# Expert weights in one transfer of 48 KB rows, with the opening and the attention laid out anew, in a two-layer decoder

## The chip, the cores and the metric

One NeuronCore of a Trainium2 chip runs the whole program in one launch. The metric is the device time in microseconds. TensorE (PE) multiplies, VectorE (DVE) and ScalarE (ACT) work element by element, GpSimd (POOL) builds constants, and SyncE (SP) issues nearly all DMAs; they meet through semaphores. 16 DMA engines move the data from HBM into the on-chip memory of 128 partitions.

## What is computed

Two layers over a stream of 256 tokens by 1024 values, all in float32:

```
for l in range(2):
    h = rms_norm(x, norm_mix[l])
    if l == 0:   # u, v, q, k, vv = split(h @ even_w_in)
        a_out = gelu(u) * (tril(W_s) @ norm(gelu(v)) + b)      # 8 groups of 64, chunks of 128 tokens
        b_out = stick_breaking_attention(q, k, vv)             # 8 heads of 64
        mix = concat(a_out, b_out) @ even_w_out
    else:        # gate_b, gate_c, h2 = split(h @ odd_w_in)
        mix = (gate_b * conv3(gate_c * h2)) @ odd_w_out
    x = x + mix
    x = x + hierarchical_moe(rms_norm(x, norm_ffn[l]), ...)
out = rms_norm(x, norm_final)
```

The attention weight of query t on key s < t is sigmoid(z_ts) times the product of (1 - sigmoid(z_tj)) over s < j < t. It is worked out as exp of z minus sums of softplus. The mixture picks one of 4 groups and in it 2 of 8 experts for each token. An expert has three weights, gate and up (1024 x 512) and down (512 x 1024), 2 MB each: `out += combine * ((silu(t @ w_gate[e]) * (t @ w_up[e])) @ w_down[e])`. All 32 experts of a layer are loaded and computed, each for up to 32 tokens gathered by rank; further blocks exist for experts with more tokens.

## The kernel before

Each engine has one program, written out by hand, and semaphores order them.

**The ring.** A ring of 9 places (`RING`) holds one weight matrix of 2 MB each, 16 KB per partition (`SLOT`). Every matrix has a number n and goes to place n % 9. SyncE issues the loads in the order of use (`fill`, `first`, `expert`, `experts`, L330 to L408). Each load waits until the matrix that held the place is used up: `gate_used`, `gu_ready` or `y_ready` for the three matrices of an expert (`used_up`). PE waits for each matrix by itself (`wait_landed`).

**The expert stage** (`moe` and `expert` of each engine). A turn is three experts (`TRI`), and 27 experts run in a hardware loop of 9 turns (`TURNS`). Expert 27 (`EARLY`) has its gate and up weights in other buffers and its down weights in `spare`, all loaded ahead. Experts 27 to 31 are written out. The last one's down matrix comes in four transfers. PE's order within an expert: gate products (L1449, 64 records), up products (64), scatter of the expert before (L1466), turning of the selection (L1472), gather for the next expert (L1478), down products (L1458, 32 records).

```
for mat, used in enumerate((gate_used, gu_ready, y_ready)):
    n = L_MOE[l] + 3 * i + mat
    sp.wait_ge(used, after(l, e - TRI))
    load(n, matrix(l, e, mat), buffer(n, mat))
```

**The mixers.** Projections use split float32: ScalarE rounds a weight to fp32r (`hi`, L530), VectorE makes the rest (`lo`, L782), and PE adds three fp32r products (L1278 for channels, L1323 for tokens, L1339 for the output). A high part lies two places back in the ring. Layer 0 starts on five pieces of the transposed x and of the first weight matrix (`PIECES`, L427 and L343), so that PE can start early. Its attention goes in two halves of four heads: `scores` (L1370), `clip` (L864), exp and ln (L613, L618), `softplus` with a mask (L870, L872), `suffixes` (L1379 to L1381, full precision), `lows` (minimum with a mask, L879), exp (L625, L626), `values` (L1392). The v branch and the gating products (L1419) run between. Four loads of the first experts wait for the mixer's end: `even_lo` and `out_half` in layer 0, `pb_ready` and `out_half` in layer 1.

Of the kernel before, what the change touches and what calls it, by code (L numbers as in the profile page):

```python
# [50 lines left out]
L_MOE = [7, 7 + PER_MOE + 8]  # L51
L_ODD = 7 + PER_MOE
L_GAIN = L_MOE[1] + PER_MOE
LAST_DOWN = L_ODD - 1
APART = [L_EVEN, L_EVEN + 1, LAST_DOWN, L_ODD]
# [3 lines left out]
SPLIT = [L_EVEN + i for i in range(7)] + [L_ODD + i for i in range(8)]  # L59

# [18 lines left out]
def trunk(nc, x_in, x_turned_in, even_w_in, even_w_out, gmlp_w_s, gmlp_b_s, columns, odd_w_in,  # L79
          odd_w_out, norm_gains, router, w_gate, w_up, w_down, norm_final, out):  # L80
    with ExitStack() as ctx:
# [21 lines left out]
        att = [scr[:, 2048 + 384 * i:2048 + 384 * (i + 1)] for i in range(4)]  # L103
# [33 lines left out]
        def temp(cols):  # L137
# [29 lines left out]
        ident, below, upto, nlin, nones, diag = (sb(n, P) for n in (  # L167
            "ident", "below", "upto", "nlin", "nones", "diag"))
        below16, ones16 = sb("below16", P, BF16), sb("ones16", P, BF16)
# [21 lines left out]
        bank = [psum[:, i, :] for i in range(8)]  # L191
        GU, YB, XB, BB = bank[4], bank[5], bank[6], bank[7]


        landed = [sem(f"landed{i}") for i in range(RING)]
        gate_used, out_half = sem("gate_used"), sem("out_half")
# [35 lines left out]
        s_ready, low_ready, a_ready = sem("s_ready"), sem("low_ready"), sem("a_ready")  # L232
# [23 lines left out]
        def slot(n):  # L256
            return ring[:, (n % RING) * SLOT:(n % RING + 1) * SLOT]
# [8 lines left out]
        def lo_slot(n):  # L266
            return slot_halves[n % RING][:, :]
# [4 lines left out]
        def used_up(n):  # L272

            for l in range(2):
# [12 lines left out]
        def is_split(n):  # L287
            return L_EVEN <= n < L_MOE[0] or L_ODD <= n < L_MOE[1]

        def wait_landed(eng, n, turns=0):  # L290

            apart = sum(n > z and n % RING == z % RING for z in APART)
            eng.wait_ge(landed[n % RING], (turns + (n // RING + 1 - apart)) * 16)
# [26 lines left out]
        def rest_entry(l, e):  # L320
            return L_MOE[l] + 3 * e - 3


# [4 lines left out]
        def _(sp):  # L328
            def load(n, src, dst):
                sp.dma_start(dst, src).then_inc(landed[n % RING], 16)  # L330
# [8 lines left out]

            def load_piece(n, src, part, landed_of):  # L340
                ks = pieces(n)[part]
                ks = slice(ks.start, ks.stop)
                sp.dma_start(wide(n)[:, ks, :], src[:, ks, :]).then_inc(landed_of[part], 16)  # L343

            def load_early(l, i, part, parts):

                w = (w_gate, w_up)[i][l, EARLY].rearrange("(p k) f -> p k f", k=K)
# [6 lines left out]
            def load_spare(l):  # L354
                if l:
                    sp.wait_ge(y_ready, after(l - 1, EARLY))
                sp.dma_start(spare, w_down[l, EARLY].rearrange("(p j) d -> p j d", p=P)).then_inc(spare_landed, 16)

            def matrix(l, e, mat):
                w = (w_gate, w_up, w_down)[mat][l, e]  # L360
                return w.rearrange("(p j) d -> p j d", p=P) if mat == 2 else w.rearrange("(p k) f -> p k f", k=K)
# [8 lines left out]
            def expert(l, b, i):  # L370
                e = b * TRI + i
                for mat, used in enumerate((gate_used, gu_ready, y_ready)):
                    n = L_MOE[l] + 3 * i + mat
                    sp.wait_ge(used, after(l, e - TRI))
                    load(n, matrix(l, e, mat), buffer(n, mat))

            def experts(l):
                first(l, 0, 0)
                if l == 0:
                    first(l, 0, 1)  # L380
                load_spare(l)
                if l == 1:
                    first(l, 0, 1)
# [1249 lines left out]
```

## Time and profile before

| | us |
|---|---|
| median of 3 runs | 1086.62 |
| lowest, highest | 1085.47, 1086.83 |
| profiled execution | 1086.43 |
| its span | 1084.3 |

| engine | busy us | share of the span |
|---|---|---|
| PE products | 814.4 | 75% |
| PE weight loads | 637.4 | 59% |
| DVE | 321.6 | 30% |
| ACT | 192.3 | 18% |
| DMA queue 1 (SyncE's loads) | | 95.9% of 16 engines |

The page gives each engine's busy time, the span in 40 slices and the chain of work that ended last. That chain holds DMA for 63% and PE for 30%. A wait named "issue" is time in which an engine waited for nothing that the profile shows. A timeline row has the start, the duration, the engine and the line, then in brackets the idle time before it and what ended it. The profiled execution took 2.1 us more than its span; that part is not in the trace.

### The profile page before, as it was taken

The page shows a single profiled execution, that of the slowest core. Times are in us where ns is not written, and L with a number is a line of the kernel's source. Part 1 is how long each engine was busy: PE and PEld are TensorE (multiplying, and loading weights), DVE is VectorE, ACT ScalarE, POOL GpSimd, SP SyncE. Part 2 cuts the span into 40 slices and gives each one's busy share as a digit, 9 for nine tenths or more (in the row PEclk, how much of TensorE's full clock was granted, in tenths as well). Part 3 has the DMA queues.
Part 4 walks back from the last instruction along what each step waited for, and adds up shares of the span by engine and source line. Part 5 has one row for each costly group of instructions (what it writes and reads, how often), then busy time and mean ns, then how long its engine had stood idle before and what let it go on. Part 6 is the DMA issues. An engine that isn't in the chain of part 4 may idle for free.

```text
span 1084.3 us, 30469 instructions
## 1 busy us (share of the span) xinstructions
PE 814.4 (75%) x13924; PEld 637.4 (59%) x13925; DVE 321.6 (30%) x801; ACT 192.3 (18%) x367; POOL 4.9 (0%) x24
## 2 busy tenths in 40 slices
PE   8999887666676766686799998966676767676864
PEld 8887665444454545464489986754454545454642
DVE  5765522111111101121177744311111111111212
ACT  5665211000000000000163331100000000000102
POOL 1000000000000000000000000000000000000000
PEclk9999999898978888888999989988978888889988
DMA  9976999999999999999998599999999999999996
GB/s 350 426 304 257 418 427 427 429 429 429 428 429 429 428 427 430 428 427 426 417 429 368 214 400 394 430 426 430 428 428 429 429 428 428 430 428 427 429 422 254
DMA packets 35872, 439.62 MB, mean 405 GB/s; under 512 B 4208, under 2 KB 4976, under 8 KB 9968
## 3 DMA queue, kind: packets, MB, share of 16 engines
q1 hardware_dynamic: 34848, 437.58, 95.9%
q10 hardware_dynamic: 976, 1.33, 0.4%
q8 instruction: 39, 0.64, 0.2%
q14 instruction: 9, 0.07, 0.0%
HBM read 437.84 MB, written 1.05 MB: 405 GB/s over the span
## 4 chain that ended last, share of the span: by engine, by line
DMA 63%; PE 30%; DVE 3%; issue 2%; ACT 1%; SPq 0%; ACTq 0%; DVEq 0%
DMA ring<-in_w_up 32%; DMA ring<-in_w_down 30%; PE psum L1278 8%; PE psum L1449 7%; PE psum L1339 4%; PE psum L1458 4%; PE psum L1323 2%; PE psum L1466 1%; PE psum L1478 1%; PE psum L1257 1%; DMA ring<-in_even_w_in 1%; PE psum L1530 1%; DVE ring_halves L782 1%; PE psum L1472 0%; PE psum L1250 0%
## 5 line engine op out<-in xcount | busy, mean ns | idle before, releaser
L1449 PE MATMUL psum<-ring,m 128*32 128x128 f32 x7936 | 310.6, 321 | 231.3 <-DMA ring<-in_w_gate 109.9
L1449 PEld LDWEIGHTS psum<-ring,m 128*32 128x32 f32 x7936 | 272.2, 130 | 277.0 <-issue 125.1
L1143 DVE TENSOR_TENSOR m<-psum,m 128x128 f32<-128x128 f32 x64 | 18.7, 292 | 575.5 <-ACT m L683 575.5
L1458 PE MATMUL psum<-ring,m 128*32 128x256 f32 x1984 | 120.8, 380 | 15.3 <-DMA ring<-in_w_down 12.1
L683 ACT ACTIVATE m<-psum 128x128 f32<-128x128 f32 x64 | 17.7, 277 | 530.1 <-PE psum L1449 530.1
L1278 PE MATMUL psum<-scr_halves,ring_halves 128*128 128x256 f32 x768 | 107.0, 286 | 4.4 <-DVE ring_halves L782 3.8
L1278 PEld LDWEIGHTS psum<-scr_halves,ring_halves 128*128 128x128 f32 x768 | 100.9, 194 | 5.0 <-DVE ring_halves L782 4.2
L1458 PEld LDWEIGHTS psum<-ring,m 128*32 128x32 f32 x1984 | 66.2, 110 | 62.1 <-issue 21.9
L1466 PE MATMUL psum<-m 32*128 32x256 f32 x1056 | 80.7, 422 | 2.1 <-DVE m L1148 1.1
L782 DVE TENSOR_TENSOR ring_halves<-ring,ring_halves 128x2048 fp32r<-128x2048 f32 (+2 forms) x37 | 68.6, 1885 | 11.6 <-ACT ring_halves L530 11.3
L1478 PE MATMUL psum<-x,m 128*32 128x256 f32 x1024 | 69.8, 385 | 2.2 <-issue 1.5
L530 ACT ACTIVATE ring_halves<-ring 128x2048 fp32r<-128x2048 f32 (+2 forms) x37 | 57.3, 1581 | 38.7 <-PE psum L1278 28.8
L1466 PEld LDWEIGHTS psum<-m 32*128 32x128 f32 x1056 | 51.3, 199 | 21.3 <-issue 14.8
L1117 DVE STREAM_TRANSPOSE m<-psum 128x256 f32<-128x256 f32 x64 | 28.8, 450 | 91.3 <-PE psum L1478 91.3
L689 ACT ACTIVATE m<-psum 128x256 f32<-128x256 f32 x62 | 23.8, 383 | 169.0 <-PE psum L1458 169.0
L1478 PEld LDWEIGHTS psum<-x,m 128*32 128x32 f32 x1024 | 27.1, 109 | 25.6 <-issue 13.3
L1126 DVE TENSOR_SCALAR m<-count,pos,cw 128x128 f32<-128x128 f32 x128 | 38.3, 342 | 1.2 <-issue 1.2
L685 ACT ACTIVATE m<-psum 128x256 f32<-128x256 f32 x64 | 24.5, 383 | 73.8 <-PE psum L1472 73.7
L1339 PE MATMUL psum<-ring_halves,aux_halves 128*128 128x512 f32 x96 | 32.7, 395 | 0.0
L1112 DVE TENSOR_SCALAR m<-count,pos,rstd 128x32 f32<-128x32 f32 x128 | 32.2, 296 | 0.8 <-DVE extra L1100 0.7
L1472 PE MATMUL psum<-ident,m 128*128 128x128 f32 x128 | 28.0, 300 | 0.0
L1120 DVE TENSOR_TENSOR m<-m,gains 128x256 f32<-128x256 f32 x64 | 27.2, 425 | 2.2
(188 smaller groups left out, 498.4 us busy)
## 6 DMA issues: line engine op xcount, KB each, us to landing
ring<-in_w_gate SPq DMA_DIRECT2D x62, 2048.0 KB, 40.5
ring<-in_w_up SPq DMA_DIRECT2D x62, 2048.0 KB, 40.7
ring<-in_w_down SPq DMA_DIRECT2D x60, 2048.0 KB, 41.1
ring<-in_odd_w_in SPq DMA_DIRECT2D x5, 2048.0 KB, 26.2
ring<-in_even_w_in SPq DMA_DIRECT2D x3, 2048.0 KB, 20.5
ring<-in_even_w_out SPq DMA_DIRECT2D x2, 2048.0 KB, 30.8
spare<-in_w_down SPq DMA_DIRECT2D x2, 2048.0 KB, 23.2
ring<-in_w_down SPq DMA_DIRECT2D x8, 512.0 KB, 37.6
```

Source lines behind the costliest of these rows:

```text
L530: act.activation(hi_slot(n)[:, c], slot(n)[:, c], ACT.Copy).then_inc(w_hi, 1)
L782: dve.tensor_tensor(lo_slot(n)[:, c], slot(n)[:, c], hi_slot(n)[:, c].bitcast(F32), ALU.subtract).then_inc(w_lo, 1)
L1112: last = dve.tensor_scalar(sel[:, t, CAP * i:CAP * (i + 1)], ranks, pos[:, bass.ds(at(e, t), 1)], rstd[:, t:t + 1], ALU.is_equal, ALU.mult)
L1117: return dve.transpose(xg[:, i, :, :], XB[:, 0:DP].rearrange("p (q k) -> p k q", k=K))
L1126: last = dve.tensor_scalar(wsel[:, t, :].rearrange("p (n c) -> p n c", n=NP), count[:, 1:CAP + 1].unsqueeze(1).to_broadcast([P, NP, CAP]), ...
L1278: return pe.matmul(bank[banks[c // 2]][:, (c % 2) * S:(c % 2 + 1) * S], w[a][:, k, P * c:P * (c + 1)], h[b][:, k, :], start=k == 0 and a + ...
L1339: last = pe.matmul(bank[2 * t + c][:, :], mix[a][:, 4 * r + j, P * t:P * (t + 1)], w[b][:, j, 512 * c:512 * (c + 1)], start=r == 0 and j = ...
L1449: last = pe.matmul(GU[CAP * part:CAP * (part + 1), lo:lo + FP], block_of(k), w_of(k)[:, FP * part:FP * (part + 1)], start=k == 0, stop=k = ...
L1458: last = pe.matmul(YB[CAP * part:CAP * (part + 1), 0:DP], hhT[:, CAP * f:CAP * (f + 1)], w[:, f, DP * part:DP * (part + 1)], start=f == 0, ...
L1466: last = pe.matmul(bank[part][:, DP * t:DP * (t + 1)], cmb[r, P * t:P * (t + 1)], yy[r, :], start=False, stop=False, skip_group_check=True)
L1472: last = pe.transpose(BB[:, P * t:P * (t + 1)], wsel[:, t, :], ident[:, :])
L1478: last = pe.matmul(XB[CAP * part:CAP * (part + 1), 0:DP], sel[:, t, CAP * i:CAP * (i + 1)], x[:, t, DP * part:DP * (part + 1)], start=t == ...
```

## The change

**Expert weights.** The three matrices of an expert lie side by side in HBM, 48 KB for each partition. The ring's places shift by two, so that an expert takes three places in a row, and one entry of the ring (`HOLE`) stays unused between the odd mixer and layer 1's experts. From the third turn on (expert 6) an expert comes in one transfer that waits for `y_ready` of the expert that held its places; PE waits once. Turns 0 and 1, expert 27 and expert 31 keep one transfer for each matrix. PE's first turn is written out ahead of its loop.

**Sources.** The pieces of x, of the first two weights of layer 0, of the first of layer 1 and of the last down matrices lie contiguous in HBM.

**Attention.** Its blocks are laid out by key block and head parity, over 512 columns, in three pieces of four heads (`LATE` is the diagonal block of the second 128 keys). The causal mask goes into the scores as a product with `ident16` and `diag16` (bf16), so the masking passes of VectorE go. The later block's softplus is split (`low_hi`, `low_lo`) and its suffix sums are fp32r products. The scores run between the two halves of vv, the suffixes between the halves of v and ahead of the last quarter of u. `hi(5)` and `lo(5)` move behind the second exp and ln.

```diff
-L_MOE = [7, 7 + PER_MOE + 8]
+L_MOE = [7, 7 + PER_MOE + 9]
+HOLE = L_ODD + 8
+def place(n):
+    return (n + 2) % RING
+def is_whole(e):
+    return FINE <= e < NE - 1 and e != EARLY
...
+            def whole(l, e, i, former):
+                sp.wait_ge(y_ready, after(l, former))
+                at = place(L_MOE[l] + 3 * i) * SLOT
+                sp.dma_start(ring[:, at:at + 3 * SLOT], expert_weights_in[l, e]).then_inc(whole_landed[third(l, i)], 16)
...
-                with sp.Fori(1, TURNS) as b:
+                for i in range(TRI):
+                    second(l, i)
+                with sp.Fori(2, TURNS) as b:
                     for i in range(TRI):
-                        expert(l, b, i)
+                        whole(l, b * TRI + i, i, b * TRI + (i - TRI))
+                for e in range(DRAIN, NE - 1):
+                    whole(l, e, (e - 1) % TRI, e - 4)
...
+                act.wait_ge(consts_ready, 1)
+                act.activation(nlin_r[:, :], nlin[:, :], ACT.Copy)
+                act.activation(nones_r[:, :], nones[:, :], ACT.Copy)
...
+                    act.wait_ge(sp_ready, 3 * g + 1)
+                    act.activation(low_hi, att[LATE], ACT.Copy).then_inc(low_hi_made, 1)
+                def weights(g):
+                    for i in (0, 1, LATE):
+                        act.wait_ge(s_ready, 3 * g + i + 1)
+                        act.activation(piece(i), score[i], ACT.Exp).then_inc(a_ready, 1)
...
-                logs(4)
+                logs(1)
+                hi(5)
+                gelu_u(0)
+                weights(1)
+                gelu_u(1)
...
+                def softplus(g):
+                    for n, i in enumerate((LATE, 0, 1)):
+                        dve.wait_ge(ln_ready, 3 * g + n + 1)
+                        dve.tensor_tensor(piece(i), score[i], piece(i), ALU.max).then_inc(sp_ready, 1)
+                    dve.wait_ge(low_hi_made, g + 1)
+                    dve.tensor_tensor(low_lo, att[LATE], low_hi.bitcast(F32), ALU.subtract).then_inc(low_lo_made, 1)
...
-                scores(0)
-                tokens(L + 2, (4, 5), vv_ready)
-                for h in range(4):
-                    suffixes(h)
-                tokens(L + 3, (6, 7), v_ready)
+                tokens(L + 2, (4, 5), vv_ready, first_scores)
+                tokens(L + 3, (6, 7), v_ready, lambda: suffixes(0))
                 values(0, 6)
                 scores(4)
-                channels(L + 4, (4, 5), u_ready)
+                channels(L + 4, (4, 5), u_ready, between=lambda: suffixes(1))
...
-                with pe.Fori(0, TURNS) as T:
+                for i in range(TRI):
+                    expert(l, 0, i)
+                with pe.Fori(1, TURNS) as T:
...
+        "expert_weights": np.concatenate([given[name].reshape(2, NE, P, SLOT) for name in ("w_gate", "w_up", "w_down")], axis=3),
```

## Rows read from the trace of the kernel before

**Rows 1.** The page: GB/s in 40 slices of the span, and the queue of instructions.

```profile
GB/s 350 426 304 257 418 427 427 429 429 429 428 429 429 428 427 430 428 427 426 417 429 368 214 400 394 430 426 430 428 428 429 429 428 428 430 428 427 429 422 254
...
q8 instruction: 39, 0.64, 0.2%
```

**Rows 2.** The chain of waits (start, us, what), layer 1's expert stage.

```profile
926.34 41.93 DMA ring<-in_w_down
...
970.39 41.94 DMA ring<-in_w_down
```

**Rows 3.** Windows: us, busy of each engine (instructions), PE's clock, DMA share, GB/s.

```profile
10.00:20.00 10.00, 7.28 (x48) 7.28 (x49) 7.76 (x13) 9.17 (x16) 0.00 (x0) 0.83 1.04 421
...
180.00:440.00 260.00, 173.26 (x3428) 126.57 (x3428) 45.09 (x144) 18.78 (x54) 0.00 (x0) 0.87 1.01 429
...
450.00:460.00 10.00, 7.38 (x130) 5.08 (x130) 2.50 (x8) 1.04 (x3) 0.00 (x0) 0.84 1.02 434
```

**Rows 4.** The chain of waits, one expert of layer 0 without a wait.

```profile
152.55 3.49 PE psum L1449 x128
...
158.49 1.73 PE psum L1458 x32
```

**Rows 5.** Timeline of SyncE (start, us, engine line op), first loop pass of layer 0.

```profile
122.70 0.35 SPq L330 DMA_DIRECT2D ring<-in_w_gate  x1
...
152.61 0.33 SPq L330 DMA_DIRECT2D ring<-in_w_down  x1
```

**Rows 6.** Timeline of TensorE, a gate product in layer 1's stage.

```profile
914.57 3.51 PE L1449 MATMUL psum<-ring,m 128*32 128x128 f32 x64 [2.38 <-DMA ring<-in_w_gate]
```

**Rows 7.** Timeline of TensorE, the ends of both expert stages.

```profile
480.88 1.93 PE L1458 MATMUL psum<-ring,m 128*32 128x256 f32 x32 [0.58 <-DMA ring<-in_w_down]
...
508.51 3.67 PE L1449 MATMUL psum<-ring,m 128*32 128x128 f32 x72 [6.08 <-issue]
...
526.71 0.85 PE L1478 MATMUL psum<-x,m 128*32 128x256 f32 x11 [1.21 <-issue]
...
527.40 2.10 PE L1458 MATMUL psum<-ring,m 128*32 128x256 f32 x31
...
541.34 0.64 PE L1458 MATMUL psum<-ring,m 128*32 128x256 f32 x8 [0.48 <-DMA ring<-in_w_down]
...
1058.02 1.93 PE L1458 MATMUL psum<-ring,m 128*32 128x256 f32 x32
...
1072.05 1.93 PE L1458 MATMUL psum<-ring,m 128*32 128x256 f32 x32 [1.22 <-DVE m L1107]
```

**Rows 8.** Timeline of ScalarE, the opening.

```profile
9.55 0.91 ACT L538 ACTIVATE scr_halves<-m,gains 128x256 fp32r<-128x256 f32 x2 [2.14 <-DMA ring<-in_even_w_in]
```

**Rows 9.** Timeline of TensorE, scores and output projection of layer 0.

```profile
35.93 1.58 PE L1370 MATMUL psum<-m 64*128 64x256 f32 x16 [0.88 <-DVE m L858]
...
87.24 0.70 PE L1339 MATMUL psum<-ring_halves,scr_halves 128*128 128x512 f32 x2
```

**Rows 10.** The chain of waits, suffix products and the v projection.

```profile
48.62 0.43 PE psum L1379 x2
...
52.14 10.91 PE psum L1323 x48
```

**Rows 11.** Timeline of ScalarE, second half of the attention.

```profile
63.65 3.70 ACT L530 ACTIVATE ring_halves<-ring 128x2048 fp32r<-128x2048 f32 x2
...
71.69 2.20 ACT L613 ACTIVATE scr<-scr 128x384 f32<-128x384 f32 x4 [1.41 <-DVE scr L864]
...
75.19 1.77 ACT L618 ACTIVATE scr<-scr 128x384 f32<-128x384 f32 x4
...
76.98 1.28 ACT L646 ACT_TABLE_LOAD   x1
```

**Rows 12.** DMA issues: out<-in, queue, count, KB each, median us to landing.

```profile
m<-in_gmlp_w_s ACTq DMA_DIRECT2D x1, 512.0 KB, 9.3
...
out<-aux SPq DMA_DIRECT2D x1, 512.0 KB, 2.7
```

More of the change, by code:

```diff
@@ L59, with rest_entry, entry, third @@
 SPLIT = [L_EVEN + i for i in range(7)] + [L_ODD + i for i in range(8)]
+def rest_entry(l, e):
+    return L_MOE[l] + 3 * e - 3
+def entry(l, e):
+    return L_MOE[l] + 3 * e if e < EARLY else rest_entry(l, e)
+def place(n):
+    return (n + 2) % RING
+def third(l, i):
+    return place(L_MOE[l] + 3 * i) // 3
+def is_whole(e):
+    return FINE <= e < NE - 1 and e != EARLY
+SINGLE = [z for z in SPLIT if z not in (L_EVEN, L_EVEN + 1, L_ODD)]
+for layer in range(2):
+    for expert in range(FINE):
+        SINGLE += [entry(layer, expert) + mat for mat in range(3) if expert < TRI or mat]
+    SINGLE += [entry(layer, NE - 1) + mat for mat in range(2)]
+SINGLE.append(L_GAIN)
+WHOLE = [(layer, expert) for layer in range(2) for expert in range(TRI, NE) if expert < FINE or is_whole(expert)]
+def single_count(n):
+    return sum(z <= n and place(z) == place(n) for z in SINGLE)
+def whole_count(l, e):
+    return sum((zl, ze) <= (l, e) and place(entry(zl, ze)) == place(entry(l, e)) for zl, ze in WHOLE)
 def pieces(n):
@@ L287, in is_split, with wait_landed @@
         def is_split(n):
[L288 to L293, printed above, removed]
+            return n in SPLIT
+        def wait_landed(eng, n):
+            eng.wait_ge(landed[place(n)], 16 * single_count(n))
         @contextmanager
@@ L368, in first, with second @@
                 fill(n, matrix(l, i, mat), buffer(n, mat))
-            def expert(l, b, i):
-                e = b * TRI + i
+            def second(l, i):
+                e = TRI + i
                 for mat, used in enumerate((gate_used, gu_ready, y_ready)):
-                    n = L_MOE[l] + 3 * i + mat
-                    sp.wait_ge(used, after(l, e - TRI))
-                    load(n, matrix(l, e, mat), buffer(n, mat))
+                    n = entry(l, e) + mat
+                    sp.wait_ge(used, after(l, i))
+                    sp.dma_start(buffer(n, mat), matrix(l, e, mat)).then_inc(landed[place(n)] if mat else whole_landed[third(l, i)], 16)
@@ L905, in even, with scale_u @@
                 dve.tensor_copy(att_out, bank[6][:, :].rearrange("p (j t) -> p j t", j=2)).then_inc(av_taken, 1)
-                clip(4)
-                lo(5)
-                softplus(4)
-                for j in range(2):
+                softplus(1)
+                def scale_u(j):
                     dve.wait_ge(u_ready, j + 1)
@@ L1293, in channels @@
                         last_product(c, K - 1, last)
+                        if between and c == 2:
+                            between()
                     return
```

262 lines of the change are left out of this document (144 added, 118 removed).

## Prediction

> **What bounds the kernel now.** I read the page's slices first. Data moves at 426 to 430 GB/s in nearly every slice of both expert stages; the slices that fall short are the opening, the token mixer of layer 0 (304, 257), the one of layer 1 (214) and the end [rows 1]. So the 32 experts of a layer, of which only three and the set-aside expert 27 can be loaded ahead, are paid at the DMA rate, and the rest of the span is what lies before the first expert and behind the last load. The chain of waits says the same: in the expert stages it holds DMA pieces with one product of 1.97 us between them, and two starts of such a pair lie 970.39 - 926.34 = 44.05 us apart, three experts, so 14.68 us each for 3 x 2048 KB = 6.29 MB, or 428.5 GB/s [rows 2]; the windows give 429 over 260 us [rows 3]. TensorE needs 158.49 + 1.73 - 152.55 = 7.67 us for one expert when it waits for nothing [rows 4], about half of that. An edit there counts only if it changes the rate, or what TensorE still has to do when the last loads land.
>
> **The steady loads, part one: the rate.** 24 experts a layer (6 to 26 and 28 to 30) come as one transfer of 48 KB rows, where three of 16 KB rows came. A row that is three times as long divides by three whatever is paid per row. How much is that? The stretch of 10 to 20 us moves mostly 4 KB rows, at 421 GB/s; I take 422, since 16 KB rows begin in it. An engine takes 8 rows of 4 KB (32,768 bytes) in 1.242 us at 422, and 8 rows of 16 KB in 4.894 us at 428.5. A line through both has 24.6 ns fixed and 26.92 bytes per ns. For 8 rows of 48 KB it gives 14.633 us instead of 14.682: 0.05 us per expert. For the 21 experts of each layer whose landing is waited for (6 to 26) that is 42 x 0.05 = **-2.2 us**. The highest long-enough window shows 434 GB/s [rows 3]; at that rate it would be 42 x (14.68 - 14.50) = -7.8 us. The lower bound is zero gain, and +2 us if the new spacing of rows in memory is a little worse; nothing in the trace has that spacing. I take the line, as it rests on two row sizes of this chip.
> The Trainium skill, "DMA: Bandwidth & Descriptors", section "Bandwidth", puts the ceiling at 435 GB/s and the cost of a packet near 10.5 ns. With these as an estimate a 48 KB row would gain about 1%, some 7 us; the 4 KB rows of this trace ran faster than such a packet cost allows (it would give about 407), so the measurement decides for the smaller term, and the page's case agrees only with the rival below on the rate.
>
> **Part two: when a transfer may start.** It now waits for the down product of the expert three before, not for gate, up and down one by one. At that time one whole expert is landing and a second is queued, 14.68 us of cover against 7.67 us of products: cost nothing. Before the first whole transfer nine matrices (44 us) are queued from 122.70 us on, to 166.7, the ninth at 152.61 [rows 5]; expert 3's down product, which releases the first whole one, ends at 160.2 [rows 4]. Unrolling the first three experts brings the code loads of a first pass again in experts 3 to 5, about 2 us each; 162.5 is still before 166.7. Without that cover each us would count.
>
> **Part three: the layer's end, a loss.** TensorE can no longer do gate and up while down lands. Before, at 480.88 us expert 26's down matrix had landed and only its down product was left; now gate, up, scatter, turn and gather (158.49 - 152.55 = 5.9 us of the 7.67 [rows 4]) come behind that landing. The wait before is longer too, some 5 us in one piece; after a wait of 2.38 us the 64 products of one matrix took 3.51 us [rows 6], where those of two take 3.49 [rows 4]: the lower of the clock's two levels. Not every wait has this, so I add 1.2 us (two thirds of the 1.7 such a start loses). TensorE is thus 7.1 us behind in experts 27 to 30. There it had no waits on loads to absorb it, but waits for its own code ("issue"): 6.08 us at 508.51, then from there to 526.71 about 6.1 us per piece of code (three pieces) [rows 7]. Expert 30 ended at 529.5 (527.40 + 2.10) and would end at 536.6; expert 31 behind it takes gate, scatter, turn, up, a hidden product's turn and down, 8.0 us: 544.6 against 542.0, **+2.6 us** in layer 0. In layer 1 expert 30 ended at 1059.95, so 1067.1 + 8.0 = 1075.1 against 1074.0 (1072.05 + 1.93): **+1.1 us**. Bounds: 0 if the lag is absorbed, +8 for both if the clock stays low through a whole expert. Layer 0's end shifts all of layer 1: the loads of the odd mixer have only 114 us of TensorE work to hide in and end in gaps, so they pass it on unchanged. The odd mixer itself keeps its products, waits and releases (the unused ring entry takes the place that expert 0's gate had, with the same wait): nothing.
>
> **The opening.** The first pieces of x and of the two first weights lie contiguous in memory; their rows stay 1, 2 and 4 KB. ScalarE waited 2.14 us for piece 2, until 9.55, and TensorE's stream of products starts behind that [rows 8]. The pieces came at well under the 421 GB/s of the next stretch, 350 in the first slice against it [rows 1]. If the source spacing causes a third of that, piece 2 lands 0.7 us earlier: **-0.7 us**; bounds 0 and -3.5 (all of it, plus the low clock after the pause). The two copies of nlin and nones on ScalarE fall into its wait for the third matrix, and GpSimd has nothing to do after its constants, so its two new copies are covered too: nothing.
>
> **The attention.** TensorE's side: the scores move behind the first half of vv, so the wait of 0.88 us before them goes [rows 9]; the suffix products (52.14 - 48.62 = 3.5 us for 2048 columns [rows 10]) become 2 full-precision ones over 512 columns (half of the columns, 1.75 us) and 8 in fp32r over 256; 48 fp32r products over 512 took 10.91 us, 0.23 each [rows 10], so 0.9, in all 2.7 us; 4 products with the mask come in, 0.45. That is 1.3 us by the time of the second scores. Second half: before, ScalarE did hi(5) (3.70 us), exp (2.20), a table load (1.28), ln (1.77), another load, waited for VectorE, and the output projection started at 87.24 [rows 9, 11]. I laid out the new order on all three engines with these durations, scaled to 512 columns. u's products run 65.1 to 73.9, suffixes to 76.6, the last quarter to 79.6, the gating ones to 81.6. VectorE no longer masks (clip and max only) and ends scale_u at 81.1. ScalarE is the late one: low_hi 73.3, hi(5) 77.1, Gelu table and half of u 79.0, Exp table 80.3, three exps 82.3, Gelu table and the other half 84.2, the first high part 84.5. Two more table switches than needed (2.6 us) sit on that path. VectorE's low part is out at 85.0, and the output projection starts there instead of at 87.24: **-2.1 us**; bounds -3.5 (the switches overlap) and 0. This passes to the end in full: the loads held for the mixer's end (issued on even_lo and out_half) start as much earlier, and no load is missing then.
>
> **The sum**, against the profiled execution (1086.43 us, span 1084.3): -2.2 + 2.6 + 1.1 - 0.7 - 2.1 = -1.3, so **1085.1 us**. The profiled run lies 0.2 us under the median of 1086.62, which I leave out.
>
> **Rivals.**
> **Code loads behind long rows (slower).** The layer's end runs on code fetched 16 KB at a time (39 packets, 0.64 MB [rows 1]) by the same 16 engines. With 16 KB rows moving, a 512 KB load on the other queue, 8 rows of 4 KB per engine, took 9.3 us, and 2.7 with nothing beside it [rows 12]: 0.8 us more per row, a little over one 16 KB row (0.61 us), so an engine alternates between queues. If a fetch must let a 48 KB row (1.83 us) pass, each costs 1.2 us more. Five fall in each end while whole experts move, with 1 us of slack: +5 us twice, **1095.1**; it decides from about 0.3 us per fetch. For it: those fetches already bound TensorE there. Against: of the 6.1 us per piece one row explains only a tenth, and only half a row is left on average. The Trainium skill, same page, section "Queues, rings and completion order", says that an engine drains a whole packet of one row's ring before it switches; that is this rival's rule, no run here shows yet whether a 48 KB row is one packet.
> **The rate rises to 434.** -7.8 in place of -2.2: **1079.5**. For it: the window of 434; against: the two row sizes.
> **The opening gains more** (its bound): **1082.3**.
> **It does not do what it says**: the 48 KB rows are cut into the old packets. The rate stays and the rest of the sum with it: **1087.3**.
>
> **How the numbers follow.** Forecast 0.36, its own range 1082.5 to 1088. Code loads 0.29; rate 0.20; opening 0.09; cut rows 0.06. A measurement of this kernel can tell 0.2% (2.2 us) from no change: faster is below 1084.4, slower above 1088.8. Of the forecast's 0.36, about 0.15 lies below 1084.4 and the rest within. Faster: 0.15 + 0.20 + 0.09 = 0.44; same: 0.21 + 0.06 = 0.27; slower 0.29. The range leaves out the lower part of the rate case with all gains together and the upper part of the code case: 1077.5 to 1098.
>
> **What would show it.** The rate over 180 to 440 us at 430 (forecast) or 433 and more; packets of the loads' queue down by about 48 x 2 x 144 = 13,800 (128 rows and an estimated 16 closing ones in each transfer saved) if a row is one packet. Output projection starting near 84.5. Starts of TensorE's code pieces at the layer's end still about 6.1 us apart, or 7 and more; expert 31's last product in layer 0 some 63.7 us behind expert 26's landing (61.1 before), or 69. I would be wrong if a whole transfer found the queue empty (a dip in the slices of the expert stages), or if ScalarE's order ended later than 85 us.

## The result: slower, with a higher load rate and two longer ends

The changed kernel takes 1089.97 us (median of 20 runs, 1086.01 to 1093.3) against 1085.95 us for the kernel before on the same chip (1083.41 to 1087.01). The ratio is 1.0038, 95% interval [1.0029, 1.0047]: 4 us slower, where I forecast 1085.1 with a range of 1082.5 to 1088. Its profiled execution took 1088.63 us, span 1086.9.

The page of the changed kernel, GB/s in 40 slices and DMA queues (packets, MB, share):

```profile
GB/s 354 428 278 313 419 426 435 434 433 432 432 434 434 432 431 434 434 434 424 414 422 292 219 399 422 438 429 432 432 434 432 432 434 432 434 432 432 432 417 130
...
q1 hardware_dynamic: 21024, 437.57, 94.8%
...
q8 instruction: 48, 0.79, 0.3%
```

The expert stages move 431 to 435 GB/s where they moved 426 to 430 [rows 1]. SyncE's queue has 13,824 packets fewer than the 34,848 of before: a 48 KB row is one packet. So the change does what it says.

The first pass of the output projection, TensorE's timeline of the changed kernel (start, us, engine, line, op, in brackets the idle time before and its cause):

```profile
84.99 0.70 PE L1402 MATMUL psum<-ring_halves,scr_halves 128*128 128x512 f32 x2 [1.18 <-DVE aux_halves L983]
```

2.25 us earlier than before [rows 9], and at the very time forecast. The windows (us, busy of PE, PEld, DVE, ACT, POOL, clock, DMA share, GB/s) of the changed kernel, to be read against [rows 3]:

```profile
180.00:440.00 260.00, 169.56 (x3484) 131.46 (x3480) 44.66 (x144) 18.82 (x54) 0.00 (x0) 0.86 1.00 432
...
720.00:1000.00 280.00, 187.19 (x3792) 146.62 (x3788) 48.28 (x154) 20.31 (x59) 0.00 (x0) 0.85 1.00 433
```

All this is gain, so the loss must lie where TensorE meets the last loads. Its chain of waits in the changed kernel (start, us, what) at the end of layer 0:

```profile
417.76 3.70 PE psum L1529 x128
...
425.84 35.38 DMA ring<-in_expert_weights
461.23 0.14 issue
461.36 6.39 PE psum L1529 x128
...
471.98 33.36 DMA ring<-in_expert_weights
505.35 2.41 issue
507.75 1.00 PE psum L1529 x14
508.75 5.44 issue
514.19 5.34 PE psum L1529 x114
```

Two starts behind a landing lie 461.36 - 417.76 = 43.60 us apart, three experts: 14.53 us each, against 14.68 [rows 2]. After that, the chain is TensorE and its waits for code, the pieces called "issue". And its timeline from expert 26 on (L1529 gate and up, L1538 down, L1546 scatter, L1558 gather), both layers:

```profile
475.89 5.37 PE L1529 MATMUL psum<-ring,m 128*32 128x128 f32 x128 [3.97 <-DMA ring<-in_expert_weights]
...
483.52 1.91 PE L1538 MATMUL psum<-ring,m 128*32 128x256 f32 x32
...
507.75 1.00 PE L1529 MATMUL psum<-ring,m 128*32 128x128 f32 x14 [4.38 <-issue]
514.19 5.34 PE L1529 MATMUL psum<-ring,m 128*32 128x128 f32 x114 [5.44 <-issue]
...
526.50 1.29 PE L1529 MATMUL psum<-ring,m 128*32 128x128 f32 x36 [1.21 <-issue]
...
538.86 2.60 PE L1538 MATMUL psum<-ring,m 128*32 128x256 f32 x32 [1.23 <-DVE m L1166]
...
1007.97 6.16 PE L1529 MATMUL psum<-ring,m 128*32 128x128 f32 x128 [5.44 <-DMA ring<-in_expert_weights]
...
1016.39 1.91 PE L1538 MATMUL psum<-ring,m 128*32 128x256 f32 x32
...
1032.53 0.85 PE L1529 MATMUL psum<-ring,m 128*32 128x128 f32 x22 [1.97 <-issue]
1033.31 1.93 PE L1546 MATMUL psum<-m 32*128 32x256 f32 x16
...
1047.16 3.83 PE L1529 MATMUL psum<-ring,m 128*32 128x128 f32 x72 [6.36 <-issue]
1052.97 2.27 PE L1529 MATMUL psum<-ring,m 128*32 128x128 f32 x56 [1.99 <-issue]
...
1065.97 1.88 PE L1538 MATMUL psum<-ring,m 128*32 128x256 f32 x28
...
1074.37 1.93 PE L1538 MATMUL psum<-ring,m 128*32 128x256 f32 x32 [1.23 <-DVE m L1166]
```

The same place in layer 1 of the kernel before, expert 26's down product (layer 0's is in [rows 7]):

```profile
1012.47 1.93 PE L1458 MATMUL psum<-ring,m 128*32 128x256 f32 x32 [0.58 <-DMA ring<-in_w_down]
```

What the reader is to see: expert 26's weights land some 5 us earlier than before in both layers (TensorE starts on them at 475.89 against 480.88, and at 1007.97 against 1012.47), and yet expert 31's last product ends at 541.46 (541.98 before) and at 1076.30 (1073.98 before). From landmarks of this kind the spans compare as follows.

| stretch | before | changed | difference |
|---|---|---|---|
| start to expert 0's first gate product | 120.54 | 119.12 | -1.4 |
| to expert 26's landing, layer 0 | 360.34 | 356.77 | -3.6 |
| to expert 31's last product | 61.10 | 65.57 | +4.5 |
| to expert 0 of layer 1 | 111.66 | 109.97 | -1.7 |
| to expert 26's landing, layer 1 | 358.83 | 356.54 | -2.3 |
| to expert 31's last product | 61.51 | 68.33 | +6.8 |
| to the end | 10.3 | 10.6 | +0.3 |

The two ends cost 11.3 us, all the rest gains 8.7; the difference is that of the spans, 2.6. The two stretches of loads give 5.9 of the gain. (The stretch between the layers is measured from a landmark that moves with code waits; I give its -1.7 no cause of its own.)

### The profile page after: what moved, and what is told of

It is laid out like the page before. It is cut to its first block, busy times and chain, and to the rows that moved or that the text cites. A ratio compares the mean times of both kernels' runs of the same rounds, so it can differ in the third digit from the quotient of the medians.

```text
span 1086.9 us, 30173 instructions
## 1 busy us (share of the span) xinstructions
PE 815.6 (75%) x13908; PEld 652.2 (60%) x13909; DVE 316.1 (29%) x783; ACT 193.5 (18%) x358; POOL 6.1 (1%) x26
## 4 chain that ended last, share of the span: by engine, by line
DMA 46%; PE 45%; issue 4%; ACT 2%; DVE 1%; SPq 0%; ACTq 0%; DVEq 0%
DMA ring<-in_expert_weights 46%; PE psum L1529 14%; PE psum L1337 8%; PE psum L1538 6%; PE psum L1402 4%; PE psum L1546 4%; PE psum L1558 3%; PE psum L1384 2%; PE psum L1552 1%; PE psum L1316 1%; PE psum L1624 1%; DMA ring<-in_even_first 1%; ACT ring_halves L580 0%; PE psum L1309 0%; PE psum L1434 0%
## 5 line engine op out<-in xcount | busy, mean ns | idle before, releaser
L1529 PE MATMUL psum<-ring,m 128*32 128x128 f32 x7936 | 310.7, 327 | 241.6 <-DMA ring<-in_expert_weights 207.9
L1529 PEld LDWEIGHTS psum<-ring,m 128*32 128x32 f32 x7936 | 289.8, 135 | 271.2 <-issue 191.7
L1538 PE MATMUL psum<-ring,m 128*32 128x256 f32 x1984 | 123.3, 382 | 3.9 <-DVE m L1166 2.5
L1538 PEld LDWEIGHTS psum<-ring,m 128*32 128x32 f32 x1984 | 65.6, 111 | 51.3 <-issue 7.0
L1546 PE MATMUL psum<-m 32*128 32x256 f32 x1056 | 80.5, 412 | 5.9 <-issue 3.9
L1558 PE MATMUL psum<-x,m 128*32 128x256 f32 x1024 | 72.9, 402 | 1.6 <-DVE m L1171 1.1
L1546 PEld LDWEIGHTS psum<-m 32*128 32x128 f32 x1056 | 49.9, 188 | 22.9 <-issue 17.4
L1558 PEld LDWEIGHTS psum<-x,m 128*32 128x32 f32 x1024 | 27.8, 113 | 26.3 <-issue 14.3
L1337 PE MATMUL psum<-aux_halves,ring_halves 128*128 128x256 f32 x96 | 27.9, 296 | 0.0
```

What stands on the lines that cost most here:

```text
L1337: return pe.matmul(bank[banks[c // 2]][:, (c % 2) * S:(c % 2 + 1) * S], w[a][:, k, P * c:P * (c + 1)], h[b][:, k, :], start=k == 0 and a + ...
L1529: last = pe.matmul(GU[CAP * part:CAP * (part + 1), lo:lo + FP], block_of(k), w_of(k)[:, FP * part:FP * (part + 1)], start=k == 0, stop=k = ...
L1538: last = pe.matmul(YB[CAP * part:CAP * (part + 1), 0:DP], hhT[:, CAP * f:CAP * (f + 1)], w[:, f, DP * part:DP * (part + 1)], start=f == 0, ...
L1546: last = pe.matmul(bank[part][:, DP * t:DP * (t + 1)], cmb[r, P * t:P * (t + 1)], yy[r, :], start=False, stop=False, skip_group_check=True)
L1558: last = pe.matmul(XB[CAP * part:CAP * (part + 1), 0:DP], sel[:, t, CAP * i:CAP * (i + 1)], x[:, t, DP * part:DP * (part + 1)], start=t == ...
```

## The experiments

Two causes stand against each other for the ends. **Lag**: TensorE waits for a whole expert, so it has all products of expert 26 ahead of it at the landing (the forecast's own term, mis-sized). **Rows**: the code fetches of the written-out experts queue behind 48 KB rows (the rival with chance 0.29). All ratios are to the kernel before, on the same chip.

**1. no_whole.** Whole experts are left out, all else of the change stays. The new ring, opening, sources and attention, with the loads and waits of before: one 16 KB-row transfer and one wait per matrix.

```diff
 def is_whole(e):
-    return FINE <= e < NE - 1 and e != EARLY
+    return False
...
-                        whole(l, b * TRI + i, i, b * TRI + (i - TRI))
+                        for mat, used in enumerate((gate_used, gu_ready, y_ready)):
+                            n = L_MOE[l] + 3 * i + mat
+                            sp.wait_ge(used, after(l, b * TRI + i - TRI))
+                            load(n, matrix(l, b * TRI + i, mat), buffer(n, mat))
```

> The changed kernel with its opening, attention, places and contiguous sources, but every expert matrix is its own transfer of 16 KB rows, with its own wait, as in the kernel before; the loop starts with turn 0 again. Theory 'lag at the end of an expert stage': what the changed kernel lost lies in the whole-expert waits alone, so only the attention (-2.2 us in the traces) and the opening (-0.2) are left: 1083.5, ratio to before 0.9978, and the last product of expert 31 is 61.1 us behind the landing of expert 26's last matrix, as before. Rival 'the opening and attention give nothing back': same as before, 1086. If the new places or sources cost something by themselves it is above 1086.

Measured: 1082.8 us (12 runs), ratio 0.9983 [0.9971, 0.9996]. The rest of the change gains 1.8 us by the ratio (3.3 by the medians; forecast 2.8), and whole experts lose 6 to 7. Its rate is that of before, and expert 31 ends 61.25 us after expert 26's landing, as before:

```profile
180.00:440.00 260.00, 174.62 (x3456) 128.53 (x3452) 45.08 (x144) 18.79 (x54) 0.00 (x0) 0.86 1.01 429
```

**2. cut_rows.** The changed kernel with its start rule and its waits for whole experts kept, but an expert comes as three transfers of 16 KB rows.

```diff
-                sp.dma_start(ring[:, at:at + 3 * SLOT], expert_weights_in[l, e]).then_inc(whole_landed[third(l, i)], 16)
+                for mat in range(3):
+                    sp.dma_start(ring[:, at + mat * SLOT:at + (mat + 1) * SLOT],
+                                 expert_weights_in[l, e][:, mat * SLOT:(mat + 1) * SLOT]).then_inc(whole_landed[third(l, i)], 16)
```

> The changed kernel with each whole expert moved by three transfers of 16 KB rows that are issued together after the same single wait; TensorE still waits for all three before the gate products. Only the row length changes. If the rate comes from the row length it falls from 433 to 428.5 GB/s, +6.2 us over 42 experts. Theory 'lag only': +6.2 in full, 1096. Theory 'code loads behind long rows': 2 to 4 us per end are won back, 1088 to 1092.

Measured: 1091.34 us (6 runs; the rows theory expected 1088 to 1092, the lag alone 1096), ratio 1.0056 [1.004, 1.0072], and the rate falls back to 428:

```profile
180.00:440.00 260.00, 173.60 (x3433) 136.22 (x3437) 42.87 (x138) 18.16 (x52) 0.00 (x0) 0.84 1.01 428
```

Its ends (landing of expert 26 to expert 31's last product) are 63.34 and 65.74 us long, where those of no_whole are 61.25 and about 61 and those of the changed kernel 65.57 and 68.33. Two things follow. The long row alone makes the rate. By the two chains the rate is worth 42 x (14.68 - 14.53) = 6.3 us, but giving it up cost only 1.4 us (2.0 by the ratios), so the 16 KB rows gave 4.3 to 4.9 us back somewhere. The ends say where: they are 2.2 and 2.6 us shorter than in the changed kernel, 4.8 in all. And against no_whole, with the same rate, cut_rows is 7.9 us slower by the ratios (8.5 by the medians), 6.8 of it in the two ends.

**3. cut_end.** Only experts 28 to 30, the last whole ones, are cut into 16 KB rows. Start and single wait stay.

```diff
+                for mat in (range(3) if isinstance(e, int) and e >= DRAIN else (None,)):
+                    c = slice(0, 3 * SLOT) if mat is None else slice(mat * SLOT, (mat + 1) * SLOT)
```

> The changed kernel with only experts 28 to 30 cut into three transfers of 16 KB rows each; they still start together on the down product of the expert three before, and TensorE still waits once for all three. Theory 'long rows delay the code fetches': what the kernel with single transfers and single waits for 28 to 30 gained over the changed kernel (5.5 us) is gained here too, 1083 to 1086. Theory 'waits': that gain came from the start rule or the single waits of 28 to 30, and this kernel stays near the changed one, 1088.5 to 1091.

(The kernel with single transfers and single waits that this speaks of is fine_end, experiment 5 here, which had been measured before.)

Measured: 1085.33 us (12 runs), ratio 0.9998 [0.9987, 1.0009]: 4.6 us under the changed kernel (4.3 by the ratios) for six experts' rows, which is what experiment 2 had left over. The transfers start as before and TensorE still waits once for all three, so the row length is what differs, and the rows theory holds for the time. When does a fetch start? The DMA queue of instructions moves 16 KB pieces; windows of 0.25 us find their starts. In the changed kernel's layer 0 they stand at 491.25, 497.75, 505.00 and from there 6.25 to 6.5 us apart; in layer 1 at 1023.75, 1029.75, 1037.25, 1044.50, then 5.75 to 6.5 apart until the loads run out; the last two gaps of the stage, with queue 1 nearly empty, are 3.9 and 3.8 us. One such window of the changed kernel (start 1037.25; packets, MB, share):

```profile
q1 hardware_dynamic: 2, 0.10, 90.8%
q8 instruction: 1, 0.02, 27.4%
```

In the kernel before the gaps between the fetches of an end run from 5.7 to 6.6 us until the last experts. So 7.25, 7.5 and 7.25 are the long ones, and they come while 48 KB rows are moving. Over about 6.25 each they make 3.3 us, some two thirds of the 4.6. The ends of all kernels together show the same: of the 26 gaps with 48 KB rows moving (the changed kernel and the three of experiments 8 to 10), 17 are 6.9 us or longer, median 7.1; of the 149 with 16 KB rows moving, 14 are, median 6.3. So long gaps exist under short rows too, but are rare there.

In cut_end's layer 1 the gaps are 5.8 to 6.7 while the loads last. In its layer 0 one gap of 8.0 us stands at 517.75, behind the cut transfers. Its ends are 67.95 and 64.47 us long, 1.5 us less in sum than the changed kernel's. Its profiled execution took 1088.4 us, 3 us above its median, and the changed kernel's 1088.63, 1.3 below its own, so the two traces do not show the gain of 4.6; it rests on the medians of 12 and 20 runs. That it comes by way of the fetches is borne out by the gaps, for about two thirds of it; the rest of the way is not shown.

**4. start_rule.** no_whole, with three transfers that start together on `y_ready`, as a whole expert's does.

```diff
-                            sp.wait_ge(used, after(l, b * TRI + i - TRI))
+                        sp.wait_ge(y_ready, after(l, b * TRI + i - TRI))
```

> The kernel with 16 KB transfers and one wait per matrix (no_whole), but from expert 6 on all three transfers of an expert are issued only when the down product of the expert three before is done. Both theories of the end expect no effect, since a whole expert and a half are queued by then: 1082.8 within 1 us, ratio to before near 0.9975. If the start rule is what costs, it comes out toward 1085 or more.

Measured: 1083.44 us (10 runs), 0.9978 [0.9965, 0.9992], against 0.9983 for no_whole. The later start costs nothing that can be measured (the two differ by 0.5 us). So the 7.9 us of cut_rows against no_whole are the wait of TensorE for the whole expert, but for one other difference: cut_rows has TensorE's first turn written out. No run separates that, but 6.8 of the 7.9 us stand in the ends, far behind it, and fine_last_turns (experiment 6) has the written-out turn and is the fastest of all.

**5. fine_end.** Experts 28 to 30 are loaded and waited for matrix by matrix; 6 to 26 stay whole.

```diff
-    return FINE <= e < NE - 1 and e != EARLY
+    return FINE <= e < EARLY
```

> The changed kernel with experts 28 to 30 as three transfers of 16 KB rows each and a wait for each; experts 6 to 26 stay whole. TensorE is behind the loads there, so when these transfers may start and what it waits for is without effect; what changes is the length of the rows that are moving while code is fetched. Theory 'code loads behind long rows': each fetch in the two ends is 0.5 to 1.2 us shorter, 2 to 4 us less per end, 1083 to 1086. Rival 'lag only': the lag of gate and up products behind expert 26 stays, within 1 us of the changed kernel, 1089 to 1091, less 0.8 us for the lower rate over six experts the other way.

Measured: 1084.49 us (12 runs), 0.9985 [0.9973, 0.9998], 0.8 us under cut_end (1.4 by the ratios), about what the measurement can tell. So for experts 28 to 30 finer waits bring little or nothing beyond the shorter rows, although TensorE does wait there for a landing at times (for expert 29 in layer 0, 3.33 us in cut_end and 5.25 in cut_rows). Most of the lag must then be made ahead of them, at the landing of expert 26.

**6. fine_last_turns.** Experts 24 to 26 as well: whole ones are 6 to 23 only, and TensorE's last turn is written out.

```diff
-    return FINE <= e < NE - 1 and e != EARLY
+    return FINE <= e < EARLY - TRI
...
-                with sp.Fori(2, TURNS) as b:
+                with sp.Fori(2, TURNS - 1) as b:
...
-                with pe.Fori(1, TURNS) as T:
+                with pe.Fori(1, TURNS - 1) as T:
...
-                for e in range(EARLY, NE):
+                for e in range(EARLY - TRI, NE):
```

> The changed kernel with whole experts only from 6 to 23; experts 24 to 26 and 28 to 30 are three transfers and three waits each, and TensorE's turn 8 is written out too. Theory 'lag': the lag is gone, the rate stays for 36 of the 48 whole experts: 1083.5 - 36 x 0.147 = 1078.2. Theory 'code loads behind long rows' expects the same, since no long row moves in the ends; it differs from the lag theory only in how much of this the kernel with single transfers for 28 to 30 has already. Rival 'written-out code is the limit' (24 to 26 now run on fetched code, some 9.7 us per expert against 14.6 of loads): no gain, if it fails to catch up, 1084 or more.

Measured: 1080.09 us (6 runs, 1079.54 to 1080.94), 0.9953 [0.994, 0.9966], 1.9 us above what was expected. It beats the kernel before by 5 us and the changed one by 10. TensorE's timeline at expert 26's landing and at the end of layer 0:

```profile
477.04 1.93 PE L1543 MATMUL psum<-ring,m 128*32 128x256 f32 x32 [0.59 <-DMA ring<-in_expert_weights]
...
504.43 3.88 PE L1534 MATMUL psum<-ring,m 128*32 128x128 f32 x67 [5.91 <-issue]
...
537.42 0.64 PE L1543 MATMUL psum<-ring,m 128*32 128x256 f32 x8 [0.40 <-DMA ring<-in_last_down]
```

The end is 538.06 - 477.04 = 61.02 us long again (61.78 in layer 1), where it was 65.57 and 68.33. This run takes away both causes, the waits and the long rows, so it shows their sum.

**7. fine_26.** As fine_last_turns, but experts 24 and 25 stay whole, 26 is fine.

```diff
-                for e in range(EARLY - TRI, EARLY):
+                for e in range(EARLY - TRI, EARLY - 1):
+                    whole(l, e, e % TRI, e - TRI)
+                for e in range(EARLY - 1, EARLY):
```

> The kernel with whole experts up to 23 and single transfers behind them (fine_last_turns), with experts 24 and 25 whole too. Rate: 4 more whole experts, 4 x 0.147 = 0.6 us less, 1079.5. Rival 'long rows delay the code fetches': TensorE's written-out code of 24 to 26 is now fetched under 48 KB rows, but it has 5 us of waiting per expert to spare there, so nothing comes of it unless the fetches of expert 26 and 27 are hit, then 1081 to 1082.

Measured: 1083.04 us (12 runs), 0.9969 [0.9957, 0.9981]: 2.9 us slower than fine_last_turns (1.7 by the ratios), not faster. Its timeline shows two things. The written-out turn waits for code from 476 us on, and these waits sum to 3.3 us before the large one.

```profile
462.89 5.37 PE L1536 MATMUL psum<-ring,m 128*32 128x128 f32 x128 [4.21 <-DMA ring<-in_expert_weights]
...
476.03 0.84 PE L1536 MATMUL psum<-ring,m 128*32 128x128 f32 x19 [0.55 <-issue]
...
479.14 1.91 PE L1545 MATMUL psum<-ring,m 128*32 128x256 f32 x32
...
482.61 0.75 PE L1536 MATMUL psum<-m 128*32 128x128 f32 x19 [0.28 <-issue]
...
488.88 1.70 PE L1545 MATMUL psum<-spare,m 128*32 128x256 f32 x25 [0.80 <-issue]
...
494.91 1.03 PE L1536 MATMUL psum<-ring,m 128*32 128x128 f32 x26 [1.69 <-issue]
...
508.36 3.66 PE L1536 MATMUL psum<-ring,m 128*32 128x128 f32 x68 [6.60 <-issue]
```

fine_last_turns has 2.16 us in that stretch. And the lag is back in part: expert 25 is whole here, its products start behind its landing at 462.89 and at the low clock (5.37 us), and TensorE reaches expert 26's down product at 479.14, 1.6 us behind the landing of that matrix (477.58); in layer 1 it is 1.6 us too. In fine_last_turns it is 0.14 us. So one whole expert ahead of the fine ones already makes TensorE late. How much of the 2.9 us is this lag and how much the long rows of experts 24 and 25 is not shown.

**8. warm.** How much of the lag is the low clock behind the long wait (5.37 and 6.16 us for 128 products in the timeline, 3.70 at full clock)? TensorE gets 16 idle products, unused, behind each down product of its loop.

```diff
+                    if not isinstance(T, int):
+                        for _ in range(WARM):
+                            pe.matmul(GU[:, 0:P], nones[:, :], nones[:, :], start=True, stop=True)
```

> The changed kernel with 16 products of nothing (128 x 128, into the gate bank, overwritten later) behind each down product inside TensorE's loop, so that the wait for the next whole expert is mostly filled. Clock part of the lag: the products of expert 26 then run at the full clock, 1.9 us less in each end, 1086.2 or 3.8 us below the changed kernel. Rival 'the clock does not matter, the lag is the moved products': 1089 to 1091. If the filling delays the gate products of the next expert it is above that.

Measured: 1097.79 us (6 runs), 1.0113 [1.0092, 1.0133]. It is neither of the two times expected; what the expectation named last happened, the filling stands in the way. TensorE's timeline of warm:

```profile
472.08 3.84 PE L1616 MATMUL psum<-nones 128*128 128x128 f32 x32
477.15 3.70 PE L1530 MATMUL psum<-ring,m 128*32 128x128 f32 x128 [1.23 <-DMA ring<-in_expert_weights]
...
484.95 3.84 PE L1616 MATMUL psum<-nones 128*128 128x128 f32 x32
488.72 1.08 PE L1530 MATMUL psum<-scr,m 128*32 128x128 f32 x32
```

In layer 0 the clock is saved (3.70); in layer 1 it isn't, the idle products end 2.89 us ahead of the landing and the 128 products take 5.37 us. And the same idle products stand at 484.95 in front of expert 27, whose weights had long been there: 3.84 us in each end, 7.7 in all; 7.8 were lost.

**9. warm_2.** None behind the third expert of a turn, so none in front of expert 27.

```diff
-                    if not isinstance(T, int):
+                    if not isinstance(T, int) and i != 2:
```

> The changed kernel with 16 idle products (nones by nones, 128x128, 3.84 us, result unused) behind the down products of the first and second expert of each turn, and none behind the third, so that nothing stands in front of expert 27. TensorE runs them while it would wait for experts 25 and 26 (and all others but the first of each turn). Clock theory: the gate and up products behind expert 26's landing took 5.0 us and more in the changed kernel and 3.7 us with warm, so the lag with which TensorE enters the end is 1.3 to 1.9 us shorter in each layer: 1086.2 to 1087.4. Rival (the lag at the low clock is not what sets the end, code fetches are): within 1 us of the changed kernel, 1089 to 1091. If the 16 products of warm did not stand in the way in its ends (my reading of its loss), this one stays slow at 1096 to 1099.

Measured: 1091.12 us (4 runs), 1.0051 [1.0031, 1.007]. 6.7 us came back, so the reading of warm's loss holds. The clock question isn't answered: with a pause of 2.89 us before expert 26 its products ran at the low clock again.

```profile
474.96 5.37 PE L1530 MATMUL psum<-ring,m 128*32 128x128 f32 x128 [2.89 <-DMA ring<-in_expert_weights]
```

**10. warm_3.** 24 idle products behind the second expert instead of 16.

```diff
-                        for _ in range(WARM):
+                        for _ in range(WARM + 8 * i):
```

> As warm_2, with 24 idle products instead of 16 behind the second expert of each turn. In warm_2 the pause ahead of expert 26 was still 2.89 us and its gate and up products still took 5.37 us; with 8 more (1.9 us) about 1 us of pause stays, and in warm a pause of 1.23 us was followed by 3.70 us. If the products behind that landing take 3.7 us here and the time they lose is passed on, each end is 1.7 us shorter: 1087.0 to 1088.5. If the code fetches take it up, or the products stay at 5.4 us, 1090 to 1092.

Measured: 1094.29 us (6 runs), 1.0079 [1.0061, 1.0098]. Both expectations missed. The clock is saved in both layers, in front of expert 27 stands nothing, and it is slower still. TensorE's timeline of warm_3, expert 26 in layer 0 and the waits for code in layer 1:

```profile
476.44 3.70 PE L1530 MATMUL psum<-ring,m 128*32 128x128 f32 x128 [1.11 <-DMA ring<-in_expert_weights]
...
1027.07 1.22 PE L1547 MATMUL psum<-m 32*128 32x256 f32 x3 [2.57 <-issue]
1049.90 2.36 PE L1530 MATMUL psum<-ring,m 128*32 128x128 f32 x40 [6.14 <-issue]
1055.88 4.92 PE L1530 MATMUL psum<-ring,m 128*32 128x128 f32 x88 [3.63 <-issue]
1069.12 0.62 PE L1530 MATMUL psum<-ring,m 128*32 128x128 f32 x10 [1.79 <-issue]
```

The waits for code sum to 13.2 us in layer 0 and 14.1 in layer 1, where the changed kernel has 11.7 and 11.9. These waits take back 1.5 and 2.2 us of the 1.7 and 2.5 won at expert 26, yet the ends came out 2.9 and 1.7 us longer than the changed kernel's. Where the rest is lost stays open: the idle products also lengthen the loop's code and may shift the written-out code against its 16 KB pieces, and no run separates this. Such a shift is in each kernel here that changes TensorE's program (no_whole, start_rule, fine_last_turns, fine_26, warm and its two variants; fine_end only adds waits), so I trust their differences to 2 or 3 us (an estimate: 1.4 to 2.9 us is what fine_last_turns and fine_26 leave unexplained). cut_end differs from the changed kernel in SyncE's program and in the numbers that TensorE's waits compare with, nothing else, so its verdict is free of this; so is cut_rows' against the changed kernel.

## Why the prediction was wrong, step by step

Two steps failed. Part three, the layer's end, stood in the sum at +3.7 us and measured +7.9: the lag was sized about right up to the start of expert 27, but not through the experts behind it. And code loads behind long rows stood in the sum at nothing, as a rival, and measured +4.3. The rate had the opposite error (-2.2 forecast, -6.3 measured), so the time came out nearer to the forecast than these steps deserve; that is luck. Without it the kernel would have been 4 us slower still.

**The rate**: right direction, too small. 14.53 us per expert, not 14.63: -6.3 us in 42 experts, not -2.2. The step that failed was the line through two row sizes. Through 16 KB rows (4.894 us for 8) and the measured 48 KB rows (14.533 us) it has 9.3 ns per row and 27.2 bytes per ns, and would give 410 GB/s for 4 KB rows. The window of the opening that I took for them shows 421 at a DMA share of 1.04 [rows 3], and 16 KB rows begin in it: too short and too mixed to carry a slope. The trace of the kernel before held a better measure, the durations of single packets: on average 160.5 ns for its 4 KB rows in that window and 614.7 ns for its 16 KB rows between 180 and 440 us. A line through these two gives 1,826 ns for 48 KB, 1.0% less than three times 614.7, so some -6 us; the changed kernel's 48 KB rows took 1,820. (A smaller slip: 42 x 0.05 is 2.1, not 2.2.) The estimate from the Trainium skill, "DMA: Bandwidth & Descriptors", section "Bandwidth", a cost per packet near 10.5 ns and so about 1%, some 7 us, agrees with this trace (9.3 ns, and 428.5 to 432.9 GB/s). The prediction set it aside for the window's rate, and that choice was wrong. It had been put down to a rival with chance 0.20, whose price (7.8) was nearly right.

**The start rule**: nothing, as forecast, and start_rule measured it. The cover was even larger than I worked out: the first whole transfer was issued at 160.21 us and landed at 185.1, while the transfer ahead of it landed only at 170.6, 10 us behind the issue.

**The layer's end, lag**: the mechanism was right and the size wrong, +3.7 forecast, +7.9 measured (cut_rows against no_whole); the prediction's upper bound was 8. The entry into the end was sized well: expert 26's down product ends 485.25 - 475.89 = 9.4 us behind the landing in layer 0 and 1016.39 + 1.73 - 1007.97 = 10.2 in layer 1, where it was 1.7 in both: 7.6 and 8.4 late, forecast 7.1. What failed is how much is absorbed in experts 27 to 31. (The following figures are of the changed kernel, so the long rows are in them.) In layer 0 expert 30 ended at 531.96, counted from the landing 7.5 us late, about as forecast, but expert 31's own work took 9.5 us, not 8.0 (its down product ran at the lower clock level for a part, 2.60 us against 1.93). In layer 1 expert 30 ended at 1065.97 + 1.88 = 1067.85, 59.9 us behind the landing, against 1059.95 - 1012.47 = 47.5 before [rows 7]: 12.4 us late, where the forecast passed on 7.1. Of the excess of 5.3, the two long fetch gaps make 2.2; another part is products at the lower clock level behind a wait for code, as the scatter at 1033.31 with 1.93 us (1.15 at full clock).

**Code loads behind long rows**: the rival with chance 0.29 happened. Its rule (an engine finishes a row before it switches to another queue's) was priced at 1.2 us per fetch, and the long gaps are 1.0 to 1.25 us longer. Its count was too high: not five but three gaps of each end lie wholly under 48 KB rows, since experts 27 and 31 come in shorter ones, and of these one (layer 0) and two (layer 1) are late by so much. So it is worth 4.3 to 4.9 us, not 10. (Nor does it decide from 0.3 us per fetch: by its own terms, 2 x (5 x 0.5 - 1) = 3, it takes 0.5 to leave the range.) The Trainium skill, same page, section "Queues, rings and completion order", states that rule for a packet. The three long gaps of the changed kernel agree with it in size; that a row is one packet shows in the count of packets.

**Opening and attention**: the output projection starts at 84.99, forecast 85.0; the stream of products in the opening starts at 12.52 us against 12.72, -0.2 instead of -0.7. (85.0 against 87.24 was a gain of 2.2; the forecast's sum took 2.1.) The way there was as laid out too: ScalarE, forecast as the late engine, ended hi(5) at 77.3 (forecast 77.1) and the last half of u at 84.1 (84.2), and VectorE's low part was out at 84.8 (85.0). Together with what they set free the new parts gain 1.8 us by no_whole's ratio (interval 0.4 to 3.1), forecast 2.8.

**The sum** with measured terms: -1.8 + 7.9 - 6.3 + 4.3 = +4.1, and the ratio says +4.1. This is not an independent confirmation, as three of the terms are differences of the same runs; what is independent is that cut_end, by the ends' rows alone, gives 4.3, and that the landmarks give 11.3 us of loss in the ends against 7.9 + 4.3 = 12.2. fine_last_turns should gain both and give up the rate of six experts, 12.2 - 0.9 = 11.3 under the changed kernel; it is 9.9 (9.2 by the ratios). 1.4 to 2.1 us are not accounted for, within what a shift of the code may do.

## What to carry to other kernels

Join loads into long rows where only the rate counts, and end that well ahead of the point where an engine must catch up with the last loads: there, short transfers with a wait each let it work while the rest lands, and here it was 10 us between whole experts to the end and whole experts up to expert 23. Look at what moves while an engine runs code that is fetched as it goes: here the fetches came 6.3 us apart (median) under 16 KB rows, 7.1 under 48 KB rows and 3.8 with the queue nearly empty. When work is pushed behind a landing, follow it to the end of the stage with the clock level of each product, and assume that nothing absorbs it until a wait on data is seen that does.

## What the runs showed that I had not expected

- The gain of a longer row does not end at 16 KB: 428.5 GB/s with rows of 16 KB, 432.9 with rows of 48 KB, which is 9.3 ns per row.
- The start of the next 16 KB piece of code depends on what queue 1 moves: 3.8 to 3.9 us behind the last one when it runs dry, 6.3 (median) under 16 KB rows, 7.1 under 48 KB rows.
- 16 idle products of 128 by 128, two records each, take 3.84 us, and they saved the clock for expert 26 where they ended 1.1 to 1.2 us ahead of the landing (3.70 us for the 128 products behind it), not where they ended 2.9 us ahead (5.37 us). The pause alone doesn't decide: in warm's layer 0 a pause of 2.80 us, at 448.00, was followed by 3.70 us.
- Saving the clock there did not shorten the run: 1.7 and 2.5 us were won at expert 26, 1.5 and 2.2 came back as longer waits for code, and the ends were longer all the same.
